# Inverse roots of the RMS norms as exp(-½ ln) on ScalarE in a two-layer decoder step

## The chip, the core and the metric

The kernel runs on one core of one Trainium2 chip. The metric is the device time of one execution in microseconds (us), as a median over runs. Engines are called by the short names of the profile: PE is TensorE's matmul, PEld its weight load, DVE is VectorE, ACT is ScalarE, POOL is GpSimd, and SP is SyncE, which here issues the weight transfers.

## What is computed

One inference step of a 2-layer hybrid decoder for 256 prompt tokens and 8 × 8 sample tokens, 320 columns in all, with a model width of 2048. Layer 0 is differential attention beside an RG-LRU; layer 1 is a short gated convolution; each layer ends in a squared-ReLU MLP. What matters here is that every RMS norm needs one over a root:

```python
def rmsnorm(x, g):
    xf = x.astype(jnp.float32)
    y = xf * lax.rsqrt(jnp.mean(xf * xf, axis=-1, keepdims=True) + RMS_EPS)
    return (y * g.astype(jnp.float32)).astype(x.dtype)

def modulated_norm(x, g, shift, scale):
    return rmsnorm(x, g) * (1.0 + scale) + shift
...
    q = rope(rmsnorm(q.reshape(bsz, t, H_ATT, 2, DH), W["q_norm"][e]), pos)
    k = rope(rmsnorm(k.reshape(bsz, t, H_ATT, 2, DH), W["k_norm"][e]), pos)
...
    o = (rmsnorm(o, W["subln"][e]) * (1.0 - lam_init)).reshape(bsz, t, W_ATT)
```

`modulated_norm` runs four times over the whole width (twice in each layer), the norms of q and k once for each of 8 heads, and the norm of the attention output `o` once for each head, for prompt and for sample.

## The kernel before, in words

The program is written out by hand for five engines. Each engine has its own list of instructions, and semaphores tie the lists together: `x.wait_ge(sem, n)` holds an engine's list until another has counted `sem` up to n. Nothing reorders; an instruction that waits holds back all that stands behind it on its engine.

**Weights.** SP loads each weight chunk (512 rows by 256 columns) into one of four slots `raw`. ACT copies it to `w_hi` (line 564, fp32r), DVE makes `w_lo = raw - w_hi` (line 954), and PE multiplies three times (hi·hi, hi·lo, lo·hi, through `mul`, line 1608). ACT's copy waits for the slot's last multiplication. The other large stream is the modulation weights (`wide_first`, `narrow`, `wide_later`): PE multiplies them with the conditioning vectors into `aux`, in small pieces placed between other work; ACT copies each finished group out (`ada_out`, line 581), PE folds it, DVE adds the bias (line 1011).

**The stages** of the profiled execution, in order: setup and the first norm with the first matrix's last columns (to about 230 us), the rest of the input projection with the RG-LRU between (to 441 us), the q/k norms and rotary (441 to 509), prompt attention (509 to 588), sample attention (to 705), the head norms inside the start of the output projection (to 745), then dense matmuls: output projection, MLP, convolution layer, MLP.

**Where a root stands**, and the names that the change touches:

- `root()` and `inverse_root()`, four times. PE sums the squares into `aux`, ACT takes the root into `rstd` (128 x 320, line 660), DVE takes the reciprocal (line 1018) and goes on to scale (line 1025). PE can start the next matrix only with scaled, split tiles, so this chain is exposed each time.
- the q/k loop, 16 tiles. In turn i ACT squares tile i (`a_sq`, line 792), takes the root of tile i-1 (`a_rt`, line 797), and copies transposed v or k tokens out of PSUM (`vtok`, `ktok`, lines 804 and 805); in every fourth turn it copies a group (line 581). DVE takes the reciprocal of a tile (`a_rr`, line 1384), applies it with the gain (`a_qn`, line 1387), and makes the rotary of the tile before (lines 1391, 1393, 1395). PE sums squares, transposes, does two chunks of modulation weights and the rotation. The tiles are double-buffered.
- the sample heads' norm, once and small (`small`, 128 x 4, lines 850 and 1496).
- the prompt heads' norms, 8 tiles of 128 x 256 (`l_g`, lines 867 and 1512). They stand among ACT's and DVE's splitting of the first four chunks of the output projection, which PE multiplies as half pairs (`half_pair`). PE's list alternates sums for the heads (`head_sums`) with half pairs.

ACT holds the tables of one set of functions at a time. The compiler puts an ACT_TABLE_LOAD ahead of an activation whose function is not in the set that is loaded. Copy, Identity, Square and Relu never need one here.

Of the kernel before, what the change touches and what calls it, by code (L numbers as in the profile page):

```python
# [10 lines left out]
ACT = mybir.ActivationFunctionType  # L11
# [3 lines left out]
D = 2048  # L15
KT = D // P
SEQ, NB, DS = 256, 8, 8
TS = NB * DS
T = SEQ + TS
NC = 1 + NB  # L20
H, DV, DH = 8, 128, 64
# [117 lines left out]
def trunk_kernel(nc, A, O):  # L139
    with ExitStack() as ctx:  # L140
# [9 lines left out]
        def at(name, offset, shape, dt=F32):  # L150
            return nc.alloc_sbuf_tensor_at(name, shape, dt, offset=offset)

        def new(name, shape, dt=F32):
            return at(name, region(4 * int(np.prod(shape[1:]))), shape, dt)

        def sem(name):
            return ctx.enter_context(nc.semaphore(name))
# [20 lines left out]
        rstd = new("rstd", [P, T])  # L178
# [21 lines left out]
        small = new("small", [P, 2, 16])  # L200
# [27 lines left out]
        a_rt = at("a_rt", RH + 24576 + 2560, [P, 2, T])  # L228
        a_rr = at("a_rr", RH + 24576 + 5120, [P, 2, T])
# [16 lines left out]
        l_g = at("l_g", RM + 4096, [P, 2, 2, T])  # L246
# [3 lines left out]
        mm = ctx.enter_context(nc.psum_tensor("mm", [P, 3, 2, 512], F32))  # L250
        aux = ctx.enter_context(nc.psum_tensor("aux", [P, 2, 512], F32))
# [3 lines left out]
        def C(name, rows=P):  # L255
            return const[0:rows, COL[name][0]:COL[name][1]]
# [5 lines left out]
        def qk_tile(i):  # L262

            return 8 + i if i < 8 else i - 8

        def tok_bank(n):

            return (mm[:, 2, 0, :], aux[:, 0, :])[n % 2]
# [7 lines left out]
        def sems(text):  # L276
            out = [sem(n) for n in text.split()]
            assert not names & set(text.split())
            names.update(text.split())
            return out if len(out) > 1 else out[0]  # L280
# [19 lines left out]
        sp_val, sp_fn = sems("sp_val sp_fn")  # L300
        ada_copied, fold_done, mod_ready = sems("ada_copied fold_done mod_ready")
        x_ready = sems("x_ready")
        sq_ready, sq_summed, norm_root, h_scaled, h_prompt, h_val, h_hi_ready, h_ready = sems(
            "sq_ready sq_summed norm_root h_scaled h_prompt h_val h_hi_ready h_ready")
        u_val, u_hi_ready, u_ready = sems("u_val u_hi_ready u_ready")
        qk_sq, qk_ms, qk_root, qk_norm, qk_rot, qk_ready = sems("qk_sq qk_ms qk_root qk_norm qk_rot qk_ready")
        tok_t, tok_ready = sems("tok_t tok_ready")
        p_score, p_max, p_exp, p_w, p_wT, p_pt, p_o, p_out = sems("p_score p_max p_exp p_w p_wT p_pt p_o p_out")
        tab_in = sems("tab_in")
        keys_in = [sem("keys_even"), sem("keys_odd")]  # L310
        values_in = [sem("values_even"), sem("values_odd")]
        s_sq, s_root, s_norm, s_back = sems("s_sq s_root s_norm s_back")
        s_kTt, s_kTe, s_prep, s_score, s_max, s_exp, s_w, s_wT, s_pte, s_o, s_out = sems(
            "s_kTt s_kTe s_prep s_score s_max s_exp s_w s_wT s_pte s_o s_out")
        o_sq, o_ms, o_root, o_ready = sems("o_sq o_ms o_root o_ready")
        gate_zero, gate_in = sems("gate_zero gate_in")
        l_conv, l_gates, l_tr, l_t, l_root, l_stage, l_rowT, l_row = sems("l_conv l_gates l_tr l_t l_root l_stage l_rowT l_row")
        g_poly, g_tanh = sems("g_poly g_tanh")
# [233 lines left out]
        def _(act):  # L552
            K, G, U, AG, AF, AW, AN = Tally(), Tally(), Tally(), Tally(), Tally(), Tally(), Tally()
            N = [0]
            fn = nc.scalar.activation
# [101 lines left out]

            def root():
                act.wait_ge(sq_summed, N[0] + 1)
                fn(rstd[:, :], aux[:, 0, 0:T], ACT.Sqrt, scale=1.0 / D, bias=C("eps")).then_inc(norm_root, 1)  # L660

            def prompt(n, b):

# [123 lines left out]
            for i in range(17):  # L787

                if i < 16:
                    if i >= 2:  # L790
                        act.wait_ge(qk_ms, i - 1)
                    fn(a_sq[:, i % 2], pj[:, qk_tile(i), :], ACT.Square).then_inc(qk_sq, 1)
                if i >= 1:
                    act.wait_ge(qk_ms, i)
                    if i >= 3:
                        act.wait_ge(qk_norm, i - 2)
                    fn(a_rt[:, (i - 1) % 2], mm[:, 1, (i - 1) % 2, 0:T], ACT.Sqrt, scale=1.0 / DH, bias=C("eps")
                       ).then_inc(qk_root, 1)
                if i != 8:

                    n = i if i < 8 else i - 1
                    tok, cols = (vtok, ktok)[n // 8], slice((n % 8) * P, (n % 8) * P + P)
                    act.wait_ge(tok_t, n + 1)
                    fn(tok[:, 0:2, cols], tok_bank(n)[:, 0:2 * P].rearrange("p (a f) -> p a f", a=2), ACT.Copy)
                    fn(tok[0:TS, 2, cols], tok_bank(n)[0:TS, 2 * P:3 * P], ACT.Copy).then_inc(tok_ready, 1)
                if i % 4 == 3:
                    ada_out(True)
# [39 lines left out]
                         accum_out=small[:, 1, 8 + n:9 + n])  # L847
            ins.then_inc(s_sq, 1)
            act.wait_ge(s_sq, 1)
            fn(small[:, 1, 12:16], small[:, 1, 8:12], ACT.Sqrt, scale=1.0 / DV, bias=C("eps")).then_inc(s_root, 1)  # L850
            def mixed(n):

                first = 4 * n if n < 2 else 16 + 4 * n
                fn(h_hi[:, 4 * n:4 * n + 4, :], pj[:, first:first + 4, :], ACT.Copy).then_inc(y_hi, 1)
# [7 lines left out]
            def rooted(i):  # L862

                act.wait_ge(o_ms, i + 1)
                if i >= 2:
                    act.wait_ge(o_ready, i - 1)
                fn(l_g[:, 1, i % 2, 0:SEQ], (mm[:, 2, 1], aux[:, 0])[i % 2][:, 0:SEQ], ACT.Sqrt, scale=1.0 / DV,
                   bias=C("eps")).then_inc(o_root, 1)

            act.wait_ge(stored, 64)  # L870
            act.wait_ge(y_val, 4)
# [63 lines left out]
        def _(dve):  # L935
            K, G, U, steps = Tally(), Tally(), Tally(), Tally()
            G.off = 2
            N = [0]
            v = nc.vector

            def step(ins):
                ins.then_inc(vec_steps, 1)
                steps.up()

            def settle():

                dve.wait_ge(vec_steps, steps.now)
# [67 lines left out]
            def inverse_root():  # L1015

                dve.wait_ge(norm_root, N[0] + 1)
                step(v.reciprocal(rstd[:, :], rstd[:, :]))  # L1018
                settle()

            def scaled(b):

# [358 lines left out]

            def qk_normed(i):
                dve.wait_ge(qk_root, i + 1)
                step(v.reciprocal(a_rr[:, i % 2], a_rt[:, i % 2]))  # L1384
                settle()
                g = V("k_norm") if i < 8 else V("q_norm")
                v.scalar_tensor_tensor(a_qn[:, i % 2], pj[:, qk_tile(i), :], g, a_rr[:, i % 2], ALU.mult, ALU.mult).then_inc(qk_norm, 1)  # L1387

# [104 lines left out]
            ada_bias(2, NB - 1)  # L1493

            dve.wait_ge(s_root, 1)
            step(v.reciprocal(small[:, 1, 12:16], small[:, 1, 12:16]))
            settle()
            v.tensor_tensor(s_kT[:, 2:4, :].rearrange("p a (n d) -> p (a n) d", n=2),
                            aux[:, 0, :].rearrange("p (n d) -> p n d", n=4),
                            small[:, 1, 12:16].unsqueeze(2).broadcast_to([P, 4, P]), ALU.mult).then_inc(s_norm, 1)  # L1500
# [8 lines left out]
            def scaled_head(i):  # L1509

                dve.wait_ge(o_root, i + 1)
                step(v.reciprocal(l_g[:, 1, i % 2, 0:SEQ], l_g[:, 1, i % 2, 0:SEQ]))  # L1512
                settle()
                v.scalar_tensor_tensor(pj[:, i, 0:SEQ], pj[:, i, 0:SEQ], subln[:, 0:1], l_g[:, 1, i % 2, 0:SEQ],
                                       ALU.mult, ALU.mult).then_inc(o_ready, 1)

# [86 lines left out]
        def _(pe):  # L1603
            K, G, R, F, KF, KW, KN = Tally(), Tally(), Tally(), Tally(), Tally(), Tally(), Tally()
            N = [0]
# [217 lines left out]
            for i in range(17):  # L1823

                if i < 16:
                    pe.wait_ge(qk_sq, i + 1)
                    if i >= 2:
                        pe.wait_ge(qk_root, i - 1)
                    mul(mm[:, 1, i % 2, 0:T], C("halves"), a_sq[:, i % 2], True, True).then_inc(qk_ms, 1)
                if i != 8:  # L1830

                    n = i if i < 8 else i - 1
                    if n >= 8:
                        pe.wait_ge(qk_ready, n - 8 + 1)
                    if n >= 2:
                        pe.wait_ge(tok_ready, n - 1)
                    tile = 16 + n if n < 8 else n
                    for tt in range(3):
                        rows = P if tt < 2 else TS
                        ins = turn(tok_bank(n)[0:rows, P * tt:P * tt + P], pj[:, tile, P * tt:P * tt + rows])  # L1840
                    ins.then_inc(tok_t, 1)
                if i < 16:
                    ada(range(2 * (i % 4), 2 * (i % 4) + 2))
                if i >= 1:
                    pe.wait_ge(qk_norm, i)
                    mul(mm[:, 0, (i - 1) % 2, 0:T], C("rot"), a_qn[:, (i - 1) % 2], True, True).then_inc(qk_rot, 1)
                if i < 16 and i % 4 == 3:
                    fold()
# [108 lines left out]
            def head_sums(*heads):  # L1957

                for i in heads:
                    pe.wait_ge(o_sq, i + 1)  # L1960
                    if i >= 2:
                        pe.wait_ge(o_root, i - 1)
                    mul((mm[:, 2, 1], aux[:, 0])[i % 2][:, 0:SEQ], C("ones"), l_g[:, 0, i % 2, 0:SEQ], True, True
                        ).then_inc(o_ms, 1)

# [112 lines left out]
```

## Time and profile before

| | |
|---|---|
| median of 3 runs | 3279.47 us |
| lowest, highest | 3272.97, 3281.08 us |
| profiled execution, its own time | 3272.87 us |
| span of the profiled execution | 3271.2 us |
| PE busy in the span | 3110.1 us, 95% |
| DVE busy | 1532.1 us, 47% |
| ACT busy | 1094.4 us, 33% |
| mean granted TensorE clock | 0.972 of full speed |

The span is from the first to the last instruction; 1.7 us lie around it. PE is busy nearly everywhere after 745 us, so what another engine does counts only where PE stands and waits for it. The chain of waits, which follows the end of the program back from releaser to releaser, shows where that is.

### The profile page before, as it was taken

What the parts mean: (1) busy time and instruction counts of PE and PEld (TensorE: products, weight loads), DVE (VectorE), ACT (ScalarE), POOL (GpSimd) and SP (SyncE); (2) the same over time, 40 slices, a digit from 0 to 9 for tenths busy, and PEclk for the clock granted to TensorE, in tenths of its full rate; (3) what the DMA queues carried; (4) which work ended last, traced back from release to release, by engine and by line L of the source; (5) the groups of instructions that cost most, each with busy time, mean ns of one, the idle gap of its engine ahead of it and who ended that gap; (6) DMA issues with size and microseconds to landing.
All of it is one profiled execution on the core that took longest, in us unless ns stands there. A gap on an engine that the chain in (4) does not pass through costs nothing.

```text
span 3271.2 us, 54812 instructions
## 1 busy us (share of the span) xinstructions
PE 3110.1 (95%) x21283; PEld 2851.7 (87%) x21283; DVE 1532.1 (47%) x2076; ACT 1094.4 (33%) x1311; POOL 29.7 (1%) x55
## 2 busy tenths in 40 slices
PE   6999986889899999999999899999899999999998
PEld 3788853459789989989989799999799999999998
DVE  3456565345534334334434554445644444444443
ACT  3334423123433233233233333333433332332332
POOL 0000000100000000000000000000000000000000
PEclk8999997889899999999999999999899999999999
DMA  9887787964574675575575344444344444444443
GB/s 301 310 276 229 239 289 273 350 242 150 165 253 161 199 243 168 185 252 170 181 242 183 124 136 147 154 148 149 116 148 149 150 150 148 148 150 151 148 148 109
DMA packets 508246, 624.37 MB, mean 191 GB/s; under 512 B 17984, under 2 KB 403777, under 8 KB 507780
## 3 DMA queue, kind: packets, MB, share of 16 engines
q1 hardware_dynamic: 500096, 595.66, 55.5%
q0 software_dynamic: 6112, 22.84, 1.9%
q10 hardware_dynamic: 1926, 4.24, 0.4%
q8 instruction: 87, 1.43, 0.2%
q14 instruction: 25, 0.20, 0.0%
HBM read 617.13 MB, written 5.54 MB: 190 GB/s over the span
## 4 chain that ended last, share of the span: by engine, by line
PE 91%; DVE 4%; DMA 3%; ACT 1%; issue 1%; SPq 0%; DVEq 0%; POOL 0%; ACTq 0%; POOLq 0%
PE mm L1608 83%; PE aux L1608 6%; DMA wide_first<-in_ada_mix_w 2%; DMA wide_later<-in_ada_mix_w 1%; DVE a_rr L1384 1%; PE mm L1727 1%; PE aux L1945 0%; DVE l_g L1512 0%; DVE rstd L1018 0%; ACT tmp L667 0%; DVE a_qn L1387 0%; DVE pj L1395 0%; DVE p_s L1411 0%; DVE a_t L1393 0%; DVE a_t L1391 0%
## 5 line engine op out<-in xcount | busy, mean ns | idle before, releaser
L954 DVE TENSOR_TENSOR w_lo<-raw,w_hi 128x1024 fp32r<-128x1024 f32 x752 | 919.4, 1225 | 1334.5 <-ACT w_hi L564 1333.1
L564 ACT ACTIVATE w_hi<-raw 128x1024 fp32r<-128x1024 f32 x752 | 795.1, 1058 | 1692.8 <-PE mm L1608 1692.6
L1608 PE MATMUL mm<-h_hi,w_hi 128*128 128x320 f32 x3712 | 1167.7, 315 | 39.5 <-DVE h_lo L1051 28.7
L1608 PE MATMUL mm<-h_lo,w_hi 128*128 128x320 f32 x3712 | 1152.3, 310 | 0.0
L1608 PE MATMUL mm<-h_hi,w_lo 128*128 128x320 f32 x3712 | 1152.3, 310 | 0.0
L1608 PEld LDWEIGHTS mm<-h_hi,w_hi 128*128 128x128 f32 x3712 | 702.3, 189 | 138.8 <-issue 111.2
L1608 PE MATMUL mm<-u_hi,w_hi 128*128 128x320 f32 x2304 | 712.0, 309 | 0.0
L1608 PE MATMUL mm<-u_lo,w_hi 128*128 128x320 f32 x2304 | 711.9, 309 | 0.0
L1608 PE MATMUL mm<-u_hi,w_lo 128*128 128x320 f32 x2304 | 711.9, 309 | 0.0
L1608 PEld LDWEIGHTS mm<-h_lo,w_hi 128*128 128x128 f32 x3712 | 702.5, 189 | 0.0
L1608 PEld LDWEIGHTS mm<-h_hi,w_lo 128*128 128x128 f32 x3712 | 702.0, 189 | 0.0
L1608 PEld LDWEIGHTS mm<-u_hi,w_hi 128*128 128x128 f32 x2304 | 432.4, 188 | 0.0
L1608 PEld LDWEIGHTS mm<-u_lo,w_hi 128*128 128x128 f32 x2304 | 432.4, 188 | 0.0
L1608 PEld LDWEIGHTS mm<-u_hi,w_lo 128*128 128x128 f32 x2304 | 432.4, 188 | 0.0
L1608 PE MATMUL aux<-wide_later,cs 128*32 128x512 f32 x512 | 95.4, 734 | 12.8 <-DMA wide_later<-in_ada_mix_w 11.3
L1608 PE MATMUL aux<-narrow,cs 128*32 128x512 f32 x704 | 94.6, 610 | 5.6 <-issue 5.6
L1248 DVE TENSOR_TENSOR u_lo<-mtmp,u_hi 128x640 f32 x64 | 52.8, 826 | 67.0 <-ACT u_hi L710 67.0
L710 ACT ACTIVATE u_hi<-mtmp 128x640 f32 x64 | 47.3, 739 | 98.6 <-DVE mtmp L1245 98.6
L1201 DVE SCALAR_TENSOR_TENSOR xT<-mm,mod,xT 128x256 f32 (+1 forms) x160 | 69.4, 475 | 0.0
L1608 PE MATMUL aux<-wide_first,cs 128*32 128x512 f32 x320 | 53.2, 651 | 16.5 <-DMA wide_first<-in_ada_mix_w 15.6
L581 ACT ACTIVATE ares<-aux 128x512 f32<-128x512 f32 x48 | 28.6, 596 | 110.4 <-PE aux L1608 108.7
L1608 PEld LDWEIGHTS mm<-const,ares 128*128 128x128 f32 x384 | 49.5, 197 | 13.0 <-issue 6.7
(272 smaller groups left out, 1212.0 us busy)
## 6 DMA issues: line engine op xcount, KB each, us to landing
raw<-in_mlp_w SPq DMA_DIRECT2D x512, 512.0 KB, 3.5
narrow<-in_ada_mlp_w SPq DMA_DIRECT2D x64, 1024.0 KB, 5.2
raw<-in_w_in_odd SPq DMA_DIRECT2D x96, 512.0 KB, 3.8
wide_first<-in_ada_mix_w SPq DMA_DIRECT2D x80, 512.0 KB, 7.5
raw<-in_w_in_even SPq DMA_DIRECT2D x80, 512.0 KB, 6.8
wide_later<-in_ada_mlp_w SPq DMA_DIRECT2D x64, 512.0 KB, 5.1
wide_later<-in_ada_mix_w SPq DMA_DIRECT2D x64, 512.0 KB, 10.7
narrow<-in_ada_mix_w SPq DMA_DIRECT2D x24, 1024.0 KB, 5.3
```

The lines of the kernel that those rows point to most:

```text
L564: fn(w_hi[:, slot], raw[:, slot], ACT.Copy).then_inc(hi_ready, 1)
L581: fn(ares[:, :], acc, ACT.Copy).then_inc(ada_copied, 1)
L710: fn(u_hi[:, bass.ds(j, 2), :], mtmp[:, r], ACT.Copy).then_inc(u_hi_ready, 1)
L954: v.tensor_tensor(w_lo[:, slot], raw[:, slot], w_hi[:, slot].bitcast(F32), ALU.subtract).then_inc(lo_ready, 1)
L1201: ins = v.scalar_tensor_tensor(x, mm[:, r, m, 0:SEQ], g, x, ALU.mult, ALU.add)
L1248: v.tensor_tensor(u_lo[:, bass.ds(j, 2), :], mtmp[:, r], u_hi[:, bass.ds(j, 2), :].bitcast(F32), ALU.subtract).then_inc(u_ready, 1)
L1384: step(v.reciprocal(a_rr[:, i % 2], a_rt[:, i % 2]))
L1608: return nc.tensor.matmul(out, lhsT, rhs, start=first, stop=last)
L1727: return nc.tensor.transpose(out, in_, const[0:rows, 0:rows])
```

## The change

Each Sqrt on ACT followed by a reciprocal on DVE becomes two activations on ACT: Ln of the same argument (same scale, same eps as bias), and Exp with a scale of -0.5. DVE's reciprocals at lines 1018, 1384, 1496 and 1512 go, with the wait behind each. Four semaphores are new (`norm_log`, `qk_log`, `s_log`, `o_log`): ACT waits for its own Ln, and PE waits for them where it waited for the root to have read a PSUM bank.

```diff
             def root():
                 act.wait_ge(sq_summed, N[0] + 1)
-                fn(rstd[:, :], aux[:, 0, 0:T], ACT.Sqrt, scale=1.0 / D, bias=C("eps")).then_inc(norm_root, 1)
+                fn(rstd[:, :], aux[:, 0, 0:T], ACT.Ln, scale=1.0 / D, bias=C("eps")).then_inc(norm_log, 1)
+                act.wait_ge(norm_log, N[0] + 1)
+                fn(rstd[:, :], rstd[:, :], ACT.Exp, scale=-0.5).then_inc(norm_root, 1)
...
                 if i >= 1:
                     act.wait_ge(qk_ms, i)
+                    fn(a_rt[:, (i - 1) % 2], mm[:, 1, (i - 1) % 2, 0:T], ACT.Ln, scale=1.0 / DH, bias=C("eps")
+                       ).then_inc(qk_log, 1)
                     if i >= 3:
                         act.wait_ge(qk_norm, i - 2)
-                    fn(a_rt[:, (i - 1) % 2], mm[:, 1, (i - 1) % 2, 0:T], ACT.Sqrt, scale=1.0 / DH, bias=C("eps")
-                       ).then_inc(qk_root, 1)
+                    act.wait_ge(qk_log, i)
+                    fn(a_rr[:, (i - 1) % 2], a_rt[:, (i - 1) % 2], ACT.Exp, scale=-0.5).then_inc(qk_root, 1)
...
-            fn(small[:, 1, 12:16], small[:, 1, 8:12], ACT.Sqrt, scale=1.0 / DV, bias=C("eps")).then_inc(s_root, 1)
+            fn(small[:, 1, 12:16], small[:, 1, 8:12], ACT.Ln, scale=1.0 / DV, bias=C("eps")).then_inc(s_log, 1)
+            act.wait_ge(s_log, 1)
+            fn(small[:, 1, 12:16], small[:, 1, 12:16], ACT.Exp, scale=-0.5).then_inc(s_root, 1)
...
-                fn(l_g[:, 1, i % 2, 0:SEQ], (mm[:, 2, 1], aux[:, 0])[i % 2][:, 0:SEQ], ACT.Sqrt, scale=1.0 / DV,
-                   bias=C("eps")).then_inc(o_root, 1)
+                fn(l_g[:, 1, i % 2, 0:SEQ], (mm[:, 2, 1], aux[:, 0])[i % 2][:, 0:SEQ], ACT.Ln, scale=1.0 / DV,
+                   bias=C("eps")).then_inc(o_log, 1)
+                act.wait_ge(o_log, i + 1)
+                fn(l_g[:, 1, i % 2, 0:SEQ], l_g[:, 1, i % 2, 0:SEQ], ACT.Exp, scale=-0.5).then_inc(o_root, 1)
...
             def inverse_root():
                 dve.wait_ge(norm_root, N[0] + 1)
-                step(v.reciprocal(rstd[:, :], rstd[:, :]))
-                settle()
...
             def qk_normed(i):
                 dve.wait_ge(qk_root, i + 1)
-                step(v.reciprocal(a_rr[:, i % 2], a_rt[:, i % 2]))
-                settle()
...
-            step(v.reciprocal(small[:, 1, 12:16], small[:, 1, 12:16]))
-            settle()
...
                 dve.wait_ge(o_root, i + 1)
-                step(v.reciprocal(l_g[:, 1, i % 2, 0:SEQ], l_g[:, 1, i % 2, 0:SEQ]))
-                settle()
```

The order of instructions moves in more than the diff shows, since the compiler's table loads are not in the source. Before, ACT's list holds 14 table loads in the whole program; with the change it holds 68. A turn of the q/k loop on ACT, before (a_sq is the squaring, a_rt the root):

```order
L792 ACTIVATE a_sq<-pj 128x320 [waits qk_ms]
L797 ACTIVATE a_rt<-mm,const 128x320 [waits qk_norm,qk_ms]
L804 ACTIVATE vtok<-mm 128x2x128 [waits tok_t]
L805 ACTIVATE vtok<-mm 64x128
L792 ACTIVATE a_sq<-pj 128x320 [waits qk_ms]
```

The same turn of the changed kernel (its lines are a few further down):

```order
L794 ACTIVATE a_sq<-pj 128x320 [waits qk_ms]
L797 ACT_TABLE_LOAD
L797 ACTIVATE a_rt<-mm,const 128x320 [waits qk_ms]
L802 ACT_TABLE_LOAD [waits qk_log]
L802 ACTIVATE a_rr<-a_rt 128x320 [waits qk_norm]
L808 ACTIVATE vtok<-mm 128x2x128 [waits tok_t]
L809 ACTIVATE vtok<-mm 64x128
L794 ACTIVATE a_sq<-pj 128x320 [waits qk_ms]
```

One activation has become two, each with a table load ahead of it: the Ln takes one set of functions, the Exp another. All 16 tiles have this pair.

Two of the prompt heads on ACT among the splits of the output projection, before:

```order
L860 ACTIVATE l_g<-pj 128x256 [waits o_ms]
L867 ACTIVATE l_g<-mm,const 128x256 [waits o_ready,o_ms]
L564 ACTIVATE w_hi<-raw 128x1024 [waits chunk_used,landed2]
L860 ACTIVATE l_g<-pj 128x256 [waits o_ms]
L867 ACTIVATE l_g<-aux,const 128x256 [waits o_ready,o_ms]
```

and with the change:

```order
L866 ACTIVATE l_g<-pj 128x256 [waits o_ms]
L873 ACT_TABLE_LOAD [waits o_ready]
L873 ACTIVATE l_g<-mm,const 128x256 [waits o_ms]
L876 ACT_TABLE_LOAD
L876 ACTIVATE l_g<-l_g 128x256 [waits o_log]
L564 ACTIVATE w_hi<-raw 128x1024 [waits chunk_used,landed2]
L866 ACTIVATE l_g<-pj 128x256 [waits o_ms]
L873 ACT_TABLE_LOAD [waits o_ready]
L873 ACTIVATE l_g<-aux,const 128x256 [waits o_ms]
```

The copy to `w_hi` that PE's next half pair needs (line 564) now stands behind two table loads and an Exp. PE's list is unchanged but for the names of two semaphores; DVE's is shorter by the reciprocals.

## Rows read from the trace of the kernel before

**Rows 1.** The page: engines' busy time, and the chain that ended last by engine.
```profile
PE 3110.1 (95%) x21283; PEld 2851.7 (87%) x21283; DVE 1532.1 (47%) x2076; ACT 1094.4 (33%) x1311; POOL 29.7 (1%) x55
PE 91%; DVE 4%; DMA 3%; ACT 1%; issue 1%; SPq 0%; DVEq 0%; POOL 0%; ACTq 0%; POOLq 0%
```

**Rows 2.** Stretches: length, busy PE, PEld, DVE, ACT, POOL; clock, DMA share, GB/s.
```profile
441.00:506.00 65.00, 48.84 (x265) 22.62 (x265) 60.13 (x77) 23.51 (x66) 2.04 (x4) 0.95 0.96 335
506.00:580.00 74.00, 52.24 (x269) 23.78 (x273) 32.34 (x91) 22.49 (x82) 4.87 (x9) 0.69 0.75 260
580.00:705.00 125.00, 109.62 (x1169) 59.01 (x1161) 33.79 (x122) 21.06 (x45) 12.64 (x24) 0.87 0.97 362
```

**Rows 3.** Timeline of the q/k loop: start, duration, engine, instruction, idle before it.
```profile
446.65 0.46 ACT L792 ACTIVATE a_sq<-pj 128x320 f32<-128x320 f32 x1
...
447.56 2.15 DVE L1384 RECIPROCAL a_rr<-a_rt 128x320 f32<-128x320 f32 x1 [3.01 <-ACT a_rt L797]
...
448.81 0.38 ACT L804 ACTIVATE vtok<-mm 128x256 f32<-128x256 f32 x1 [1.29 <-PE mm L1727]
449.09 0.26 ACT L805 ACTIVATE vtok<-mm 64x128 f32<-64x128 f32 x1
449.25 0.46 ACT L792 ACTIVATE a_sq<-pj 128x320 f32<-128x320 f32 x1
449.61 0.51 ACT L797 ACTIVATE a_rt<-mm,const 128x320 f32<-128x320 f32 x1
...
453.32 0.60 ACT L581 ACTIVATE ares<-aux 128x512 f32<-128x512 f32 x1 [0.72 <-PE aux L1608]
...
503.58 2.15 DVE L1384 RECIPROCAL a_rr<-a_rt 128x320 f32<-128x320 f32 x1
...
509.02 0.81 PE L1608 MATMUL mm<-pj 64*128 64x128 f32 x4 [1.50 <-DVE pj L1395]
```

**Rows 4.** Timeline: two table loads, the activation behind each, and one ahead.
```profile
47.49 0.60 ACT L581 ACTIVATE ares<-aux 128x512 f32<-128x512 f32 x1 [8.97 <-PE aux L1608]
48.10 1.28 ACT L660 ACT_TABLE_LOAD   x1
49.40 0.53 ACT L660 ACTIVATE rstd<-aux,const 128x320 f32<-128x320 f32 x1
...
504.96 1.28 ACT L815 ACT_TABLE_LOAD   x1
...
512.78 0.40 ACT L815 ACTIVATE p_s<-p_s,small 128x128 f32<-128x128 f32 x1 [6.54 <-DVE small L1415]
```

**Rows 5.** Timeline of ACT from the sample heads' root to the first prompt head.
```profile
706.03 0.30 ACT L850 ACTIVATE small<-small,const 128x4 f32<-128x4 f32 x1
706.23 1.25 ACT L854 ACTIVATE h_hi<-pj 128x1280 fp32r<-128x1280 f32 x1
...
708.86 0.40 ACT L860 ACTIVATE l_g<-pj 128x256 f32<-128x256 f32 x1
709.16 1.04 ACT L564 ACTIVATE w_hi<-raw 128x1024 fp32r<-128x1024 f32 x1
710.11 0.45 ACT L867 ACTIVATE l_g<-mm,const 128x256 f32<-128x256 f32 x1
```

**Rows 6.** Timeline: a head's reciprocal on DVE, and PE's half pairs behind idle time.
```profile
711.53 1.75 DVE L1512 RECIPROCAL l_g<-l_g 128x256 f32<-128x256 f32 x1
...
729.74 0.63 PE L1608 MATMUL mm<-h_hi,w_hi 128*128 128x320 f32 x1 [3.58 <-DVE w_lo L954]
...
742.67 0.63 PE L1608 MATMUL mm<-h_hi,w_hi 128*128 128x320 f32 x1 [5.76 <-DVE w_lo L954]
```

**Rows 7.** Stretches, as in rows 2: a half pair at either granted clock.
```profile
714.90:721.00 6.10, 6.10 (x42) 5.92 (x40) 6.03 (x10) 1.73 (x3) 0.00 (x0) 1.00 0.25 86
...
729.70:733.00 3.30, 3.26 (x12) 3.26 (x13) 3.27 (x3) 0.00 (x0) 0.00 (x0) 0.50 0.49 159
```

**Rows 8.** By line: the full-width norm's reciprocal, and ACT's idle time before the root.
```profile
L1018 DVE RECIPROCAL rstd<-rstd x4: 2153/2154/2154, 50.0 to 2341.0; 128x320 f32<-128x320 f32 x4
...
  PE aux L1608: 20.6, 3
```

More of the change, by code:

```diff
@@ L302, in trunk_kernel @@
         x_ready = sems("x_ready")
-        sq_ready, sq_summed, norm_root, h_scaled, h_prompt, h_val, h_hi_ready, h_ready = sems(
-            "sq_ready sq_summed norm_root h_scaled h_prompt h_val h_hi_ready h_ready")
+        sq_ready, sq_summed, norm_log, norm_root, h_scaled, h_prompt, h_val, h_hi_ready, h_ready = sems(
+            "sq_ready sq_summed norm_log norm_root h_scaled h_prompt h_val h_hi_ready h_ready")
         u_val, u_hi_ready, u_ready = sems("u_val u_hi_ready u_ready")
-        qk_sq, qk_ms, qk_root, qk_norm, qk_rot, qk_ready = sems("qk_sq qk_ms qk_root qk_norm qk_rot qk_ready")
+        qk_sq, qk_ms, qk_log, qk_root, qk_norm, qk_rot, qk_ready = sems("qk_sq qk_ms qk_log qk_root qk_norm qk_rot qk_ready")
         tok_t, tok_ready = sems("tok_t tok_ready")
@@ L311, in trunk_kernel @@
         values_in = [sem("values_even"), sem("values_odd")]
-        s_sq, s_root, s_norm, s_back = sems("s_sq s_root s_norm s_back")
+        s_sq, s_log, s_root, s_norm, s_back = sems("s_sq s_log s_root s_norm s_back")
         s_kTt, s_kTe, s_prep, s_score, s_max, s_exp, s_w, s_wT, s_pte, s_o, s_out = sems(
             "s_kTt s_kTe s_prep s_score s_max s_exp s_w s_wT s_pte s_o s_out")
-        o_sq, o_ms, o_root, o_ready = sems("o_sq o_ms o_root o_ready")
+        o_sq, o_ms, o_log, o_root, o_ready = sems("o_sq o_ms o_log o_root o_ready")
         gate_zero, gate_in = sems("gate_zero gate_in")
@@ L1827, in _ @@
                     if i >= 2:
-                        pe.wait_ge(qk_root, i - 1)
+                        pe.wait_ge(qk_log, i - 1)
                     mul(mm[:, 1, i % 2, 0:T], C("halves"), a_sq[:, i % 2], True, True).then_inc(qk_ms, 1)
@@ L1961, in head_sums @@
                     if i >= 2:
-                        pe.wait_ge(o_root, i - 1)
+                        pe.wait_ge(o_log, i - 1)
                     mul((mm[:, 2, 1], aux[:, 0])[i % 2][:, 0:SEQ], C("ones"), l_g[:, 0, i % 2, 0:SEQ], True, True
```

## The prediction, made before the changed kernel was run

> **What bounds the kernel now.** I read the page's busy times first, then the chain that ended last, then the timeline at the four places where a root is taken. PE is busy 95% of the span and makes up 91% of the chain; DVE has 4% of it, DMA 3%, ACT 1% [rows 1]. So the change can count only in the exposed places. Of DVE's 4%, the reciprocals are the largest part: in the q/k stage (441 to 506 us) DVE is busy 60.1 of 65 us, while ACT is busy 23.5 [rows 2]. There the turn is DVE's: from the second reciprocal to the sixteenth, 447.56 to 503.58 us, 14 turns take 56.02 us, 4.00 us each [rows 3]. The reader is to see two things: DVE is the pacer there, and ACT has room, 4.00 us a turn less about 1.5. The question is whether what is put on ACT fits into that room.
>
> **A table load's price.** The changed order has 68 table loads where there were 14: Ln and Exp stand in different sets, so each of the 29 pairs reloads twice. The price is in the trace: the activation ahead starts at 47.49 and takes 0.60, the load starts at 48.10 and takes 1.28, the next activation starts at 49.40 [rows 4]. From the end of one activation to the start of the next it is 1.31 us, so I take 1.30 to 1.31 per load. A load ahead of an activation that waits goes first and does not wait itself: the one at 504.96 had ended when its Exp was released at 512.78 [rows 4]. So a load is free if ACT would idle anyway, and a load between a Ln and its Exp is always on the way from sum to result.
>
> The Trainium skill (ScalarE: Activation LUTs, section What ACT_TABLE_LOAD costs) gives a load about 1.28 us, and adds a drain of about 1.38 us, 2.66 us for each switch. On the load itself the trace agrees (1.28); of the drain it shows nothing but 0.01 to 0.02 us at either side.
>
> **Full-width norms, four.** Removed from the chain: a reciprocal of 2.15 us [rows 8] and 0.03 between engines. Added: a load of 1.31 and an Exp. An Exp of this shape has no row without pointer operands; its nearest is the Square from SBUF, 0.46, and the root from PSUM, 0.51 to 0.53 [rows 3, 4]. I take 0.51. So 2.18 becomes 1.31 + 0.51 + 0.02 = 1.84: a gain of 0.34 each. In three of them ACT idles before the root, 20.6 us in all [rows 8], so the Ln's own load is hidden; if that cover were gone it would cost 1.31 each. In the first norm a load stands on the way already and stays [rows 4]. Sum: **-1.4 us** (0 to -1.6; the first one's 0.34 may be lost to the transfers behind it).
>
> **The q/k loop.** DVE's turn falls from 4.00 to about 1.85 (less 2.15). ACT's turn becomes, by start-to-start steps: Square 0.46 and 0.01; load 1.30; Ln 0.51, and 0.03 until its own semaphore is seen; load 1.30; Exp 0.42 until the copy starts (0.51 less the overlap of 0.1 that the rows show); first copy 0.28; second copy 0.16 [rows 3, 4]. Together 4.47 us. Every fourth turn adds a group's copy, 0.49 (0.60 less the overlap), 0.12 a turn. ACT then needs **4.59 us a turn** and nothing it waits for is late: the sums and transposes for a tile are made a turn earlier, and PE has 48.8 busy of 65 us [rows 2]. ACT becomes the pacer, and DVE waits for it. The beginning is bound by the first modulation chunks, as before: the Square at 446.65 stays [rows 3]. From there: Square 0.47, load 1.30, Ln 0.54, load 1.30, Exp 0.42, so the first copy of turn 2 starts at 450.7. Thirteen turns of 4.47 and three group copies of 0.49 bring turn 15's copies to 510.3. After these come its copies and group copy (1.04), load, Ln, load, Exp (1.30 + 0.54 + 1.30 + 0.51): the last Exp ends at 515.0. In the kernel before, the last reciprocal ends at 505.73 and PE goes on at 509.02, 3.29 later [rows 3]; that tail (gain, two rotaries) is the same. PE goes on at 518.3. Sum: **+9.3 us** (with 0.1 us a turn either way, +7.8 to +10.8). The load for prompt attention's Exp goes away, but it was hidden [rows 4].
>
> **Is it given back later?** The sample stage is bound by transfers (DMA share 0.97 at 362 GB/s), the prompt stage before it is not (0.75) [rows 2]. Transfers can run ahead by eight chunks only, and with a quarter of the prompt stage's DMA time free these are full when the sample stage starts. More time in the q/k stage cannot fill them further. I take nothing back.
>
> **Sample heads' root.** The Ln starts at 706.03 like the root. Removed: nothing that the next copy (`h_hi` at 706.23 [rows 5]) waits for. Added ahead of that copy on ACT: the rest of the Ln 0.1, a load 1.30, the small Exp 0.2. **+1.6 us** for all that follows; the small reciprocal that DVE saves (under 0.2) is not on it.
>
> **Prompt heads, 8, among the splits.** Before, DVE paces: the first half pair of the last four starts at 742.67, after PE idled 5.76 us for `w_lo` [rows 6]. Now I add ACT's list from the small Ln's end (706.34) to the end of the split for that half pair. Load and small Exp 1.5; three large copies of 1.17 are 3.5 (1.25 less overlap); eight squares of 0.31 are 2.5; five splits of 0.95 are 4.7; eight pairs, each load, Ln, load, Exp at 1.30 + 0.49 + 1.30 + 0.37, are 27.7 [rows 4, 5]. That is 39.9 us. ACT waits once in it, for head 6's sum, which PE makes after its fourth half pair; walked through by the same prices this is 2.3 us. So the split ends at about 748.5, `w_lo` takes 1.22, PE starts at 749.8: +7.1 against 742.67, of which 1.6 is the sample root above. All loads but one are on the way, because ACT's list has no idle time to hide them. A head's reciprocal of 1.75 [rows 6] and the load with Exp between Ln and result (1.30 + 0.47) are equal, so DVE's relief buys nothing. **The clock.** PE's third half pair now starts after some 3.6 us of waiting. In the rows a half pair after a wait of 3.58 us ran at a granted clock of 0.5, the 1.2 GHz level, where one without a wait ran at 1.00, 2.4 GHz [rows 6, 7]. 24 matmuls then take up to 6.2 us instead of 3.6, of which ACT's queue hides about half; I add 1.3 (0 to 2.6). Sum: **+8.4 us** with the sample root (+5.5 to +10).
>
> **Sum.** -1.4 + 9.3 + 8.4 = +16.3 us. The profiled execution took 3272.87 us and would take 3289.2. It was the low end of the three runs (3272.97 to 3281.08, median 3279.47); a median should be met by a median, so I forecast 3279.5 + 16.3 = **3295.8 us**, slower by 0.5%. About 0.3%, 9.8 us, is what a measurement of this kernel can tell from no change.
>
> **Rivals.**
> A. *One set for both functions* (faster). If the chip needed no reload between Ln and Exp, ACT's turn would be 2.0 us and the q/k loop would be bound by its transfers, 1.05 MB a turn, 3.0 us near 350 GB/s: -14 us. The norms would gain 1.65 each, -6.6, and the heads would lose up to 8 of DVE's 31 us. About -29: 3250. It decides at 2.0 us for the two loads of a turn: under that ACT's turn is below DVE's old 4.00. Against it: the built order has both loads, and in the trace of before every load of the order was executed, 14 of 14. 3%. In a sentence of its own: the Trainium skill (ScalarE: Activation LUTs, section on table sets) says that Ln then Exp costs one load, since one set holds both; by that rule this rival holds, and no row shows that set in use.
> B. *A load costs more where the loads follow each other* (slower by far). In the rows each load has a long stretch without one behind it; in the loop there is one after every activation. If each then held ACT for twice what rows 4 show, 1.31 us more, the 27 loads of the loop's last 13.5 turns and the 14 of the heads on the way would add 54 us: 3350. Nothing in the rows speaks for it. 3%. The drain named above is the skill's case for it, and would give much the same.
> C. *The price is paid where nobody waits* (within 0.3%). If the eight chunks are not full when the sample stage starts, the longer q/k stage gives back up to 8 x 0.52 MB at 362 GB/s, 11.6 us: +4.7, 3284. Or the q/k loads overlap ACT's waits. Against it: the free DMA time in the prompt stage, and a list on ACT with no waits. 14%.
> D. The forecast, 80%, itself mostly above 9.8 us: of it 76 points slower, 3 same by noise, 1 faster by noise.
>
> Range: C's end and noise of the median below, 3284; above, the bounds of the loop (+1.5), the heads (+1.6) and noise of some 5 us over a median of 3296, plus clock effects: 3308. Outside are A, B and a part of C. Slower 0.79, same 0.17, faster 0.04.
>
> **What the changed profile would show.** 68 loads on ACT, 1.28 us each. In the q/k loop, DVE waiting for `a_rr` of ACT each turn, and 4.6 us from Exp to Exp. PE's first score matmul near 518. Between 706 and 750 us ACT nearly without idle time, and PE's wait for `w_lo` before the last four half pairs longer than 5.76. The time from sum to scale in a full-width norm down by a third of a microsecond. I am wrong if the turn stays near 4.0 (loads overlapped), if it is over 5 (a drain), or if the sample stage starts 9 us later and ends less than 9 us later.

## The result

The changed kernel takes 3286.12 us (median of 20 runs, 3278.95 to 3291.12), the kernel before 3275.52 us (20 runs, 3271.65 to 3281.08): 10.6 us more, ratio 1.0033 with a 95% interval of 1.0026 to 1.0039. Two later comparisons of the same pair gave +16.1 us (1.0051, 1.0038 to 1.0065) and +10.6 us (1.0038, 1.0023 to 1.0053). The ratios are not those of the two medians; in us they say +10.8, +16.7 and +12.4. It is slower, by a third to half of a per cent.

The page of the changed kernel, busy times and the chain that ended last, to be held against [rows 1]:

```profile
PE 3117.4 (95%) x21283; PEld 2856.5 (87%) x21283; DVE 1477.3 (45%) x2047; ACT 1177.4 (36%) x1394; POOL 29.6 (1%) x55
...
PE 90%; ACT 3%; DMA 3%; DVE 2%; issue 1%; SPq 0%; DVEq 0%; ACTq 0%; POOL 0%; POOLq 0%
```

DVE is 55 us less busy, ACT 83 us more. In the chain they have changed places: DVE 4 to 2%, ACT 1 to 3%.

The q/k loop and prompt attention as stretches, to be held against [rows 2]:

```profile
441.00:518.00 77.00, 54.76 (x271) 26.23 (x272) 28.27 (x64) 71.94 (x116) 1.70 (x3) 0.89 0.83 290
518.00:590.00 72.00, 50.39 (x276) 22.97 (x274) 31.45 (x89) 22.47 (x81) 5.11 (x10) 0.72 0.79 276
```

ACT (the fourth busy figure) is busy 72 of 77 us, DVE 28. One turn on ACT's timeline, to be held against [rows 3]:

```profile
461.79 0.36 ACT L808 ACTIVATE vtok<-mm 128x256 f32<-128x256 f32 x1
462.05 0.26 ACT L809 ACTIVATE vtok<-mm 64x128 f32<-64x128 f32 x1
462.21 0.46 ACT L794 ACTIVATE a_sq<-pj 128x320 f32<-128x320 f32 x1
462.69 1.28 ACT L797 ACT_TABLE_LOAD   x1
463.98 0.53 ACT L797 ACTIVATE a_rt<-mm,const 128x320 f32<-128x320 f32 x1
464.58 1.28 ACT L802 ACT_TABLE_LOAD   x1
465.88 0.47 ACT L802 ACTIVATE a_rr<-a_rt 128x320 f32<-128x320 f32 x1
466.25 0.37 ACT L808 ACTIVATE vtok<-aux 128x256 f32<-128x256 f32 x1
```

No row has idle time before it. From copy to copy it is 4.46 us, of which 2.57 are table loads. DVE now waits for ACT in all 16 turns:

```profile
L1391 DVE SCALAR_TENSOR_TENSOR a_qn<-pj,vec,a_rr x16: 550/552/552, 447.9 to 516.9; 128x320 f32<-128x320 f32 x16
its engine sat idle before it (us, times) until:
  ACT a_rr L802: 48.2, 16
```

The heads, against [rows 6]: PE's third, fourth and fifth half pairs and what they waited for.

```profile
734.14 0.42 PE L1608 MATMUL mm<-h_hi,w_hi 128*128 128x320 f32 x1 [2.50 <-DVE w_lo L962]
...
742.86 0.42 PE L1608 MATMUL mm<-h_hi,w_hi 128*128 128x320 f32 x1 [4.07 <-DVE w_lo L962]
...
756.62 0.64 PE L1608 MATMUL mm<-h_hi,w_hi 128*128 128x320 f32 x1 [7.58 <-DVE w_lo L962]
```

**Where the time went.** I cut each profile at these events: ACT's root or Ln of the first norm; the first q/k square; PE's first prompt score; DVE's first key copy of the sample stage; ACT's small root or Ln of the sample heads; PE's fifth half pair; the root or Ln of the second norm. In us, with two profiles of the kernel before and three of the changed one (the later ones are from the experiments below):

| stretch | before | changed |
|---|---|---|
| start to the first norm's root or Ln | 49.4, 49.6 | 52.7, 53.6, 52.8 |
| q/k square to first prompt score | 70.4, 71.1 | 78.7, 79.7, 78.9 |
| prompt attention | 79.0, 79.9 | 76.0, 79.6, 78.5 |
| sample attention | 118.0, 117.9 | 118.0, 117.9, 117.6 |
| heads (small root to fifth half pair) | 36.6, 36.7 | 42.5, 42.5, 42.5 |
| rest of the first output projection | 109.1, 109.1 | 109.4, 109.5, 109.6 |
| third norm, root or Ln to PE's first product | 9.45 | 9.04 |

Two stretches carry the loss in every profile: the q/k loop with +8.3 (79.1 less 70.8, the means) and the heads with +5.9. The first 50 us hold no changed instruction and still differ.

### The profile page after: what moved, and what is told of

The parts are those of the page before. It is cut to its first block, busy times and chain, and to the rows that moved or that the text cites. A ratio compares the mean times of both kernels' runs of the same rounds, so it can differ in the third digit from the quotient of the medians.

```text
span 3282.5 us, 54866 instructions
## 1 busy us (share of the span) xinstructions
PE 3117.4 (95%) x21283; PEld 2856.5 (87%) x21283; DVE 1477.3 (45%) x2047; ACT 1177.4 (36%) x1394; POOL 29.6 (1%) x55
## 4 chain that ended last, share of the span: by engine, by line
PE 90%; ACT 3%; DMA 3%; DVE 2%; issue 1%; SPq 0%; DVEq 0%; ACTq 0%; POOL 0%; POOLq 0%
PE mm L1608 83%; PE aux L1608 6%; DMA wide_later<-in_ada_mix_w 2%; DMA wide_first<-in_ada_mix_w 1%; PE mm L1727 1%; ACT L797 1%; ACT L802 0%; PE aux L1945 0%; ACT tmp L669 0%; ACT w_hi L564 0%; DVE p_s L1415 0%; ACT a_rt L797 0%; ACT a_rr L802 0%; DVE h_lo L1057 0%; DVE p_s L1437 0%
## 5 line engine op out<-in xcount | busy, mean ns | idle before, releaser
L1254 DVE TENSOR_TENSOR u_lo<-mtmp,u_hi 128x640 f32 x64 | 52.8, 826 | 67.0 <-ACT u_hi L712 67.0
L712 ACT ACTIVATE u_hi<-mtmp 128x640 f32 x64 | 47.3, 739 | 98.6 <-DVE mtmp L1251 98.6
```

The source lines that it names most:

```text
L712: fn(u_hi[:, bass.ds(j, 2), :], mtmp[:, r], ACT.Copy).then_inc(u_hi_ready, 1)
L1254: v.tensor_tensor(u_lo[:, bass.ds(j, 2), :], mtmp[:, r], u_hi[:, bass.ds(j, 2), :].bitcast(F32), ALU.subtract).then_inc(u_ready, 1)
```

## Experiments

**1. The changed kernel again.** No edit.

> The changed kernel once more, for a second profile of it. Theory L (ScalarE's list with its table loads paces the q/k loop and the heads): from the first q/k square to the first prompt score 78.7 us again (+8.3), from the sample heads' root to PE's fifth half pair 43.8 us again (+5.9), within 0.3 us each, since nothing in them is left to chance. What differed elsewhere in the first pair of profiles (+3.3 us in the first 50 us, -3.1 in prompt attention, -1.6 in the first MLP) is not the change's and comes out otherwise this time. Rival G (given back): the longer q/k stage makes prompt attention shorter, 76.0 us again where before has 79.0. In sum L gives +12 (8.3 + 5.9 - 1.7 of the norms), G gives +9.

Measured: 3289.83 us against 3273.71 (16 runs), +16.1. The q/k stage took 79.7 us, the heads 42.5, prompt attention 79.6. The heads were on the figure (the expectations count from the table load ahead of the root or Ln, 1.3 us earlier than the table: 43.8 for 42.5, 37.9 for 36.6); the q/k stage was a microsecond off it, more than the 0.3 I allowed. The granted clock tells of prompt attention. First the changed kernel's first profile, then the one of this run, over that stage (columns as in rows 2):

```profile
520.15:596.11 75.96, 54.41 (x312) 26.52 (x312) 30.54 (x87) 24.78 (x85) 4.27 (x8) 0.74 0.81 281
```

```profile
522.26:601.86 79.60, 58.31 (x312) 29.22 (x312) 30.53 (x88) 24.79 (x85) 4.27 (x8) 0.69 0.77 269
```

The same 312 matmuls took 54.4 us of PE at a granted clock of 0.74 and 58.3 at 0.69. PE's 3.9 us less cover the stage's 3.6 us. So the 3 us that seemed to be given back after the q/k loop belong to one execution and its clock, and not to the change.

**2 and 3. The parts alone.** In the first, the full-width and head norms are as before and only the q/k loop is changed; in the second, only the head norms.

> Only the q and k norms are changed; full-width norms and head norms are as before. Theory L: q/k loop 4.58 us a turn, +8.3 us to the first prompt score, heads as before (37.9 us), in all +8.3. Rival G: prompt attention is shorter by 3 us when the q/k loop is the long one, so +5.3 in all.

> Only the head norms are changed (the small one of the samples and the eight of the prompt). Theory L: q/k loop as before (4.00 us a turn), heads 43.8 instead of 37.9 us, in all +5.9. If the heads' price depended on what the q/k loop left behind (clock, transfers), it would be another figure; half of it or less would mean that.

Measured: q/k alone 3285.01 us, +11.3 (1.0032, 1.0020 to 1.0044); its q/k stage 80.2 us, its heads 36.5, its prompt attention 78.7. Heads alone 3280.04 us, +6.3 (1.0023, 1.0014 to 1.0032); q/k stage 69.6 us, heads 42.5, prompt attention 78.6. Each stretch moves with its own edit and with no other, and prompt attention took the same behind the long loop (78.7) as behind the short one (78.6).

**4. One table set.** The changed kernel with an explicit load of the set that holds Ln and Exp both, after the first Tanh and ahead of the q/k loop. With that set active the compiler puts no load before either function: 11 loads in the program instead of 68.

```diff
+            def table_set(n):
+                nc.scalar.add_instruction(mybir.InstLoadActFuncSet(name=nc.get_next_instruction_name(), ins=[], outs=[],
+                                                                   act_func_set_id=n))
...
 then_inc(c_tanh, 1)
+            table_set(6)
             rows = 0
...
+            table_set(6)
             act.wait_ge(pair_free, 46)
             for i in range(17):
```

> The change, but with one explicit load of the table set that holds both Ln and Exp after the first Tanh and again ahead of the q/k loop; the 56 reloads between Ln and Exp are gone. Theory L: with the loads the loss goes and DVE's relief comes out: the q/k turn falls to about 3.0 us (its 1.05 MB of transfers), -14 us; heads -6, the sample heads' root -1.2, the four full-width norms -1.7 each and -1.3 more in the first, -8; in all -29 us. Rival R (reciprocals on DVE were cheap cover, not the bound): no gain beyond a few us, since ACT's second activation is still there. If the loads were not what costs, it would be near the changed kernel, +11.

Measured: **3245.95 us, -27.8 us** against before (0.9916, 0.9902 to 0.9929), the fastest kernel here. All its table loads, by line:

```profile
L784 ACT ACT_TABLE_LOAD x4 | 5.1, 1283 | 0.1
L779 ACT ACT_TABLE_LOAD x4 | 5.1, 1283 | 0.1
L558 ACT ACT_TABLE_LOAD x2 | 2.6, 1283 | 0.0
L601 ACT ACT_TABLE_LOAD x1 | 1.3, 1283 | 5.3 <-issue 5.3
```

The q/k stage of before, and then of this kernel (columns as in rows 2):

```profile
438.61:509.02 70.41, 51.11 (x272) 23.58 (x272) 63.09 (x84) 24.85 (x69) 2.54 (x4) 0.93 0.95 331
```

```profile
438.21:494.25 56.04, 50.50 (x272) 22.87 (x272) 29.91 (x68) 31.12 (x84) 2.55 (x4) 1.00 1.04 385
```

It is 14.4 us shorter, and a third thing bounds it: DVE and ACT are idle for nearly half of it, the DMA engines are full, and PE is busy 50.5 of 56.0 us. A full-width norm's Ln and Exp, and PE's first product after it:

```profile
831.36 0.53 ACT L665 ACTIVATE rstd<-aux,const 128x320 f32<-128x320 f32 x1 [6.91 <-PE aux L1614]
831.92 0.47 ACT L667 ACTIVATE rstd<-rstd 128x320 f32<-128x320 f32 x1
```

```profile
839.12 0.60 PE L1614 MATMUL mm<-h_hi,w_hi 128*128 128x320 f32 x1 [6.25 <-DVE h_lo L1063]
```

That is 7.76 us from Ln to product, where before had 9.45 and the changed kernel 9.04. The heads took 32.9 us instead of 36.6 from the small Ln on, and the load ahead of it, 1.3 us, is gone too: 5.0 in all, where I had expected 7.2. So the idea behind the change, off DVE and onto ACT, pays for itself; the reloads were the whole of the loss and more.

**5. The full-width norms alone.** Head and q/k norms as before.

> Only the four full-width norms are changed. Theory L: each is 0.41 us shorter from root to PE's first product (9.03 instead of 9.45, since a load and an Exp of 0.47 stand where a reciprocal of 2.15 stood), the other loads are hidden in ScalarE's idle time; -1.6 us in all, which no median here can tell from nothing; the profile can. If the hidden loads were not free, each norm would be 0.9 us longer.

Measured: 3272.24 us, -2.6 (0.9993, 0.9983 to 1.0004), which can't be told from nothing. The profile can. The third norm on ACT, and PE's first product, in the kernel before and then in this one:

```profile
1868.59 0.53 ACT L660 ACTIVATE rstd<-aux,const 128x320 f32<-128x320 f32 x1 [6.84 <-PE aux L1608]
```

```profile
1878.04 0.60 PE L1608 MATMUL mm<-h_hi,w_hi 128*128 128x320 f32 x1 [9.48 <-DVE h_lo L1051]
```

```profile
1869.40 0.53 ACT L660 ACTIVATE rstd<-aux,const 128x320 f32<-128x320 f32 x1 [5.54 <-PE aux L1608]
1869.94 1.28 ACT L662 ACT_TABLE_LOAD   x1
1871.24 0.47 ACT L662 ACTIVATE rstd<-rstd 128x320 f32<-128x320 f32 x1
```

```profile
1878.44 0.61 PE L1608 MATMUL mm<-h_hi,w_hi 128*128 128x320 f32 x1 [9.07 <-DVE h_lo L1051]
```

9.04 us instead of 9.45, as expected. ACT's idle time before the Ln is 5.5 us here and was 6.8 before: the first load sits in it and costs nothing.

**6. One more load a turn.** The changed kernel with a redundant load ahead of the Ln's in the q/k loop.

```diff
+                    table_set(0)
+                    table_set(5)
                     fn(a_rt[:, (i - 1) % 2], mm[:, 1, (i - 1) % 2, 0:T], ACT.Ln, scale=1.0 / DH, bias=C("eps")
```

> The changed kernel with one more table load in each q/k turn (a redundant one ahead of the Ln's), nothing else. Theory L: ScalarE's list is the pacer there, so every turn is longer by exactly a load, 1.30 us: the turn goes from 4.58 to 5.88, the q/k stage from 79 to 98.5 us (15 turns' worth; the first may hide behind the first transfers), and nothing is given back: +35 against before. If loads were partly hidden by waits, the turn would grow by less; with a price for loads in a row (the prediction's rival B) by more than 1.31.

Measured: 3309.79 us, +34.9 (1.0109, 1.0094 to 1.0123). The q/k stage took 98.6 us. The Exp of each turn, and the 32 explicit loads:

```profile
L808 ACT ACTIVATE a_rr<-a_rt x16: 469/469/470, 442.4 to 530.1; 128x320 f32<-128x320 f32 x16
```

```profile
L558 ACT ACT_TABLE_LOAD  x32: 1283/1283/1283, 438.0 to 526.9; - x32
```

From first to last Exp 87.7 us for 15 turns, 5.85 each, where the changed kernel has 4.61 (447.3 to 516.4). A load adds 1.24 us a turn, its own length but for 0.04, and a row of two is twice one. That settles the price, and rules out rival B of the prediction.

**7. The loads without the Exp.** The kernel before, root and reciprocal untouched, with two loads ahead of each root.

```diff
+                    table_set(5)
+                    table_set(3)
                     fn(a_rt[:, (i - 1) % 2], mm[:, 1, (i - 1) % 2, 0:T], ACT.Sqrt, scale=1.0 / DH, bias=C("eps")
```

> The kernel before (root on ScalarE, reciprocal on VectorE) with two table loads ahead of each root in the q/k loop, and no Exp. By ScalarE's sum alone the turn would be 4.05 us against 4.00, +1 us in all. By the loop of waits it is more: gain on VectorE, rotation, sum and transposes on PE, token copy, square, two loads, root on ScalarE, reciprocal come to 8.56 us for two turns, so 4.3 to 4.4 a turn: +4.5 to 5.5 us. The two figures tell whether the room on ScalarE that the prediction spoke of (2.0 us of loads) was really there.

Measured: 3290.51 us, +15.7 (1.0047, 1.0035 to 1.0059); q/k stage 84.4 us, +14, where I had expected +5.5 at most. Both figures were too low. The two-turn loop of waits is there as reckoned. Gain on DVE, token copy, square, loads, root:

```profile
471.42 0.55 DVE L1393 SCALAR_TENSOR_TENSOR a_qn<-pj,vec,a_rr 128x320 f32<-128x320 f32 x1
...
473.74 0.38 ACT L810 ACTIVATE vtok<-mm 128x256 f32<-128x256 f32 x1 [0.60 <-PE mm L1733]
...
474.18 0.46 ACT L796 ACTIVATE a_sq<-pj 128x320 f32<-128x320 f32 x1
474.65 2.57 ACT L558 ACT_TABLE_LOAD   x2
...
477.24 0.53 ACT L803 ACTIVATE a_rt<-mm,const 128x320 f32<-128x320 f32 x1
```

```profile
479.99 0.55 DVE L1393 SCALAR_TENSOR_TENSOR a_qn<-pj,vec,a_rr 128x320 f32<-128x320 f32 x1
```

From gain to gain two turns later it is 8.57 us, as the 8.56 of the expectation. But over the whole loop the turn is 4.87 us (449.3 to 522.4 for 15; the kernel before has 4.12 by the same cut). I had left out that a group's copy also waits for PE in this loop (0.51 us idle and 0.60 of work every fourth turn), and that PE, idle longer, runs some of its steps at the lower clock: rotation and sum take 2.50 us from 504.17 in this profile's chain of waits, 1.34 from 485.78. The chain's two pieces, and the two stretches with their granted clock (columns as in rows 2):

```profile
485.78 1.34 PE mm L1614 x4
...
504.17 2.50 PE mm L1614 x4
```

```profile
485.70:487.20 1.50, 1.42 (x7) 1.04 (x7) 1.47 (x5) 0.73 (x2) 0.00 (x0) 0.99 1.05 395
504.10:506.70 2.60, 2.53 (x6) 1.64 (x7) 2.34 (x5) 1.52 (x2) 0.00 (x0) 0.50 0.75 201
```

I have not separated these two. What follows is plain all the same: the room on ACT was no room. The reloads with the reciprocal kept cost more (+14) than the reloads with the reciprocal gone and an Exp added (+8.3).

**8. The kernel before again.** No edit.

> The kernel before once more, for a second profile. If the first 50 us and prompt attention vary by themselves, the first norm's root starts nearer 53 us than 49.4 (as in all four profiles since), and prompt attention is 78 to 80 us; the q/k stage is 69.5 to 70.5 us and the heads 36.6 us, as in the profiles that kept them.

q/k stage 71.1 us, prompt attention 79.9, heads 36.7: near the figures expected, the q/k stage half a microsecond over. But the first norm's root started at 49.6 us, not near 53. Over all eleven profiles it started between 49.4 and 53.6, once at 49.4 with the change in (experiment 6) and at 53.4 and 52.8 with the first norm changed or not (experiments 5 and 3). So the change does not set it.

**9. The changed kernel a third time.**

> The changed kernel a third time, since the first comparison gave +10.6 us and the second +16.1, and the parts alone sum to +15 (11.3 + 6.3 - 2.6). By the parts (theory L) it is +12 to +17, with a q/k stage of 78.5 to 80 us and heads of 42.5; the first 50 us, prompt attention and the first MLP differ by 2 to 4 us without the change and make the spread. If the first comparison's figure was the right one and something is given back, it is +9 to +12.

Measured: 3285.74 us against 3275.14, +10.6; q/k stage 78.9 us, heads 42.5, prompt attention 78.5. The medians' difference is under the range by the parts and inside the one that I had set for "something is given back"; the ratio, 1.0038, is +12.4 us and inside the range by the parts. The stretches of the profile are those of the parts, and none of them shows where anything would be given back.

## Why the prediction was right, and where it was not

**The direction and the mechanism held.** The forecast was slower by 16.3 us; measured were 10.6, 16.1 and 10.6. The time, 3286.1 us, is within 3284 to 3308, and the ratio 1.0033 is just over the bound of 0.3%. That it fell inside the range owes something to luck: the forecast was too high both in its base and in its terms, and the low end of the range had been set by rival C, which did not happen.

**The level.** Of the 9.7 us between forecast and median, 4.0 are the start: the three runs shown of before had a median of 3279.47, 20 runs have 3275.52. A median of three runs that lay 8 us apart was too thin to add to. The other 5.7 are in the sum, 16.3 against 10.6, of which the heads are 2.5.

**The price of a load** (1.30 to 1.31 from end to start, no drain): right. In the changed kernel the load at 462.69 begins 0.02 after the square and the Ln 0.01 after it. Experiment 6 confirms it with loads in a row.

**Full-width norms:** forecast -0.34 each, measured -0.41; the Exp took 0.47, not 0.51. The hidden loads were hidden (experiment 5).

**The q/k loop:** forecast 4.47 us a turn, 4.59 with the group copies, +9.3. Measured 4.46, 4.61, and +8.3 from the mean of three profiles against two. The stage has two pieces that behave differently. From the square of turn 2 to the end of the last reciprocal or Exp it is 59.1 us in both profiles of before and 68.5, 68.4 and 68.3 in the three changed ones: +9.3, the forecast to 0.1. From the first square to that of turn 2, which I had taken as fixed, it is 8.0 and 8.8 before, 6.9, 8.0 and 7.3 changed, and in the parts 7.1 where this loop is as before (experiment 3) and 8.9 where it is changed (experiment 2). That piece varies without regard to the edit, and the missing microsecond lies in it.

**Given back later:** I took nothing. Behind the longer loop prompt attention took 76.0, 79.6, 78.5 and 78.7 us, behind the loop as before 79.0, 79.9, 78.6 and 79.1: a microsecond between the means, inside the spread. Behind the two longest loops (experiments 6 and 7) it took 81.7 both times, more and not less; no run says why. Sample attention, where rival C wanted the time back, took 117.6 to 118.0 us in all profiles of before and changed. The first pair, with its 76.0 against 79.0 us in prompt attention, would have misled anyone who stopped there.

**The sample root:** forecast +1.6. The copy behind it starts 1.72 after the Ln (714.08 to 715.80), where it started 0.20 after the root [rows 5]: +1.5.

**The heads** are the term that was mis-sized: +8.4 with the sample root, measured +5.9, in every profile that had it. Two steps failed. ACT's one wait in its list was put at 2.3 us and was 0.51:

```profile
748.64 0.47 ACT L873 ACTIVATE l_g<-mm,const 128x256 f32<-128x256 f32 x1 [0.51 <-PE mm L1608]
```

In all the list took 40.9 us from the small Ln's end at 714.38 to the end of the split at about 755.3, against 42.2 forecast; its other figures came to 40.4, half a microsecond over their 39.9. And the clock, +1.3: I took it that PE's third half pair, behind some 3.6 us of waiting, would run at the lower level, as the fourth did in [rows 6, 7]. It waited 2.50 us and did not; the fourth, behind 4.07 us, ran in part at the lower level, but it had done so before too:

```profile
734.10:738.40 4.30, 4.26 (x27) 4.19 (x28) 0.49 (x1) 4.10 (x7) 0.00 (x0) 1.00 0.38 125
...
742.80:748.60 5.80, 5.74 (x27) 5.69 (x28) 1.89 (x3) 5.25 (x7) 0.00 (x0) 0.71 0.27 90
```

**What is left open.** The parts alone, by medians, sum to 11.3 + 6.3 - 2.6 = +15.0 us, and the stretches by profiles to +13.0 (8.3 + 5.9 + 0.4 of the output projection - 1.6 of the norms). With +9.3 for the loop, if its beginning is left out as chance, the stretches give +14.0. Two of three comparisons of the whole say +10.6 by the medians. Each interval reaches 2 to 5 us to either side, and the stretches without an edit vary by 2 to 4 us between executions, so these don't contradict one another, but no run here shows which is nearer.

**Rival A** (one set for both) was given 3% for the kernel as built, and rightly: its 54 extra loads were executed. As a kernel of its own (experiment 4) it came out at -27.8 us where -29 was reckoned, by its own terms: q/k loop -14.4 of -14, norms -1.7 of -1.65 each, and the heads -5.0 where it had "up to 8". The Trainium skill (ScalarE: Activation LUTs, section Table sets: the hidden batching unit) says that Ln then Exp costs one load, since one set has both. With the set chosen by hand the trace agrees: two loads for 29 pairs. With the loads left to the compiler it does not: each function was served from a set of its own, 58 loads.

## What to carry to other kernels

Count the table loads of the built program before moving a function to ScalarE: here two functions that alternate cost two loads a pair until one set served both, and a load was 1.28 us of ScalarE that hid only where the engine would have idled before a wait. If a set with both exists, load it by hand ahead of the stage. An engine that is half idle need not have room: its idle time may be waits inside a loop through other engines, and then each microsecond added lengthens the loop. And before explaining 3 us in a stage, take the same kernel's profile again.

## What was not expected of the hardware

Two loads ahead of a root cost 14 us in the q/k loop with DVE's reciprocal in place, 5 us more than loads and Exp without it. And the same code took 49.4 to 53.6 us to reach the first norm, and 76.0 to 81.7 us for the same prompt attention, with the granted clock from 0.74 down to 0.68.
